# Decode attention: which queues load the paged cache (SP and POOL together, or SP alone)

## The reference, cut to what matters

```python
def mla_sample(x, cache_ckv, cache_kpe, page_table, ...):
    past_ckv = cache_ckv[page_table].reshape(B, -1, MLA_KV_LORA)   # 16 pages of 128 x 256 per batch
    past_kpe = cache_kpe[page_table].reshape(B, -1, MLA_ROPE)      # 16 pages of 128 x 64 per batch
    ...
    s = (einsum('bthr,bkr->bhtk', q_lat, all_ckv) + einsum('bthd,bkd->bhtk', q_pe, all_kpe)) * MLA_SCALE
    p = softmax(where(key_idx <= q_idx, s, -inf))
    o_lat = einsum('bhtk,bkr->bthr', p, all_ckv)
```

## Time and profile before

| | |
|---|---|
| time, median of 3 runs | 2721.86 us (2720.53 to 2725.43) |
| the profiled execution: its time / its span | 2732.0 us / 2730.3 us |
| mean granted TensorE clock | 0.938 |
| PE busy | 2497.6 us (91%) |
| DVE / ACT / POOL busy | 1053.8 us (39%) / 783.3 us (29%) / 1011.8 us (37%) |
| DMA, mean over the span | 76 GB/s |

### The profile page before, as it was taken

One profiled execution on the slowest core, in us unless ns is written; L12 is line 12 of the kernel. 1 busy time (PEld: TensorE's weight loads), 2 busy tenths in 40 slices (PEclk: granted clock), 3 DMA queues, 4 the chain that ended last, 5 costly groups with the idle time before them and its releaser, 6 DMA issues.

```text
span 2730.3 us, 45462 instructions
## 1 busy us (share of the span) xinstructions
PE 2497.6 (91%) x17472; PEld 2350.1 (86%) x17472; DVE 1053.8 (39%) x1953; ACT 783.3 (29%) x1323; POOL 1011.8 (37%) x596
## 2 busy tenths in 40 slices
PE   7999997799899699999979999979989776999996
PEld 6999997784457699999969999978988676999996
DVE  5333115576232633321163331145676446333213
ACT  4222223214332332222242222233221124222221
POOL 5333334320312343334343333443575024333342
PEclk9999998899998799999989999988989587999998
DMA  3222222120641132222212222222212211222221
GB/s 121 85 85 77 79 85 66 35 94 1 195 130 47 39 93 81 80 81 79 72 62 82 80 84 77 80 62 71 60 49 78 77 54 47 85 83 82 76 81 60
DMA packets 66584, 208.52 MB, mean 76 GB/s; under 512 B 8268, under 2 KB 19021, under 8 KB 66094
## 3 DMA queue, kind: packets, MB, share of 16 engines
q1 hardware_dynamic: 63406, 196.58, 23.3%
q0 software_dynamic: 3072, 10.49, 1.4%
HBM read 199.22 MB, written 7.82 MB: 76 GB/s over the span
## 4 chain that ended last, share of the span: by engine, by line
PE 84%; DVE 10%; issue 3%; POOL 2%; ACT 1%; DMA 0%; POOLq 0%; SPq 0%; DVEq 0%; ACTq 0%
PE psum L1389 24%; PE psum L1391 23%; PE psum L1390 23%; DVE h L919 2%; DVE x_lo L902 2%; DVE y_ffn L915 1%; PE psum L1648 1%; PE psum L1827 1%; PE psum L1704 1%; PE psum L1817 1%; PE psum L1583 1%; PE psum L1632 1%; PE psum L1777 1%; DVE work L910 1%; POOL w_lo L769 1%
## 5 line engine op out<-in xcount | busy, mean ns | idle before, releaser
L769 POOL TENSOR_TENSOR w_lo<-raw,w_hi 128x1024 fp32r<-128x1024 f32 x331 | 799.4, 2416 | 1353.5 <-ACT w_hi L467 1353.3
L1389 PE MATMUL psum<-x_hi,w_hi 128*128 128x288 f32 x3568 | 1077.6, 302 | 67.2 <-DVE x_lo L902 40.4
L1391 PE MATMUL psum<-x_hi,w_lo 128*128 128x288 f32 x3568 | 1065.0, 298 | 0.0
L1390 PE MATMUL psum<-x_lo,w_hi 128*128 128x288 f32 x3568 | 1064.7, 298 | 0.0
L1389 PEld LDWEIGHTS psum<-x_hi,w_hi 128*128 128x128 f32 x3568 | 683.7, 192 | 81.8 <-DVE x_lo L902 33.2
L1390 PEld LDWEIGHTS psum<-x_lo,w_hi 128*128 128x128 f32 x3568 | 684.0, 192 | 1.5
L1391 PEld LDWEIGHTS psum<-x_hi,w_lo 128*128 128x128 f32 x3568 | 682.9, 191 | 0.0
L467 ACT ACTIVATE w_hi<-raw 128x1024 fp32r<-128x1024 f32 x331 | 347.1, 1050 | 347.7 <-PE psum L1391 332.3
L1389 PE MATMUL psum<-gu_hi,w_hi 128*128 128x288 f32 x1408 | 418.7, 297 | 9.2 <-DVE gu_lo L953 9.2
L1391 PE MATMUL psum<-gu_hi,w_lo 128*128 128x288 f32 x1408 | 417.4, 296 | 0.0
L1390 PE MATMUL psum<-gu_lo,w_hi 128*128 128x288 f32 x1408 | 417.2, 296 | 0.0
(11 more groups left out here) (236 smaller groups left out, 2110.9 us busy)
## 6 DMA issues: line engine op xcount, KB each, us to landing
raw<-ffn_in SPq DMA_DIRECT2D x176, 512.0 KB, 3.6
raw<-ffn_out SPq DMA_DIRECT2D x64, 448.0 KB, 3.3
raw<-ffn_out SPq DMA_DIRECT2D x32, 512.0 KB, 3.5
raw<-gla_in SPq DMA_DIRECT2D x25, 512.0 KB, 3.6
cache<-cache SPq DMA_DIRECT2D x64, 160.0 KB, 3.1
cache<-cache POOLq DMA_DIRECT2D x64, 160.0 KB, 3.2
raw<-mla_wo SPq DMA_DIRECT2D x8, 512.0 KB, 3.6
raw<-gla_wo SPq DMA_DIRECT2D x8, 512.0 KB, 3.7
```

Source lines behind the costliest of these rows:

```text
L769: pool.tensor_tensor(w_lo[slot][:, :], raw[slot][:, :], w_hi[slot][:, :].bitcast(F32), ALU.subtract).then_inc(s_lo, 1)
L1389: pe.matmul(out, wh, xh, start=start, stop=False)
L1390: pe.matmul(out, wh, xl, start=False, stop=False)
L1391: return pe.matmul(out, wl, xh, start=False, stop=stop)
```

## The change

SP issues all four pages of each group and batch; the call on POOL goes, and with it the semaphores `s_cache_p`. TensorE waits for one semaphore that counts four pages instead of two that count two each. Nothing else in the order of any engine is changed.

```diff
@@ load_pages @@
-        def load_pages(eng, u0, landed, lo, hi):
+        def load_pages(eng, u0):
...
                     for b in (2 * bp, 2 * bp + 1):
-                        with eng.Fori(lo, hi) as i:
+                        with eng.Fori(0, 4) as i:
                             page = eng.value_load(table[0:1, bass.ds(PAGES * b + 4 * g + i, 1)], min_val=0,
                                                   max_val=N_POOL - 1)
                             eng.dma_start(cache[b % CACHES][:, 4 * g + i, :],
-                                          io["cache"][page]).then_inc(landed[b % CACHES][g], 16)
+                                          io["cache"][page]).then_inc(s_cache[b % CACHES][g], 16)
@@ SP, mla @@
-                load_pages(sp, u0, s_cache, 0, SP_PAGES)
+                load_pages(sp, u0)
@@ POOL, mla @@
-                load_pages(pool, first_unit[st], s_cache_p, SP_PAGES, 4)
@@ TensorE, transpose_pages @@
-                    pe.wait_ge(s_cache[b % CACHES][g], 16 * SP_PAGES * (b // CACHES + 1))
-                    pe.wait_ge(s_cache_p[b % CACHES][g], 16 * (4 - SP_PAGES) * (b // CACHES + 1))
+                    pe.wait_ge(s_cache[b % CACHES][g], 64 * (b // CACHES + 1))
```

More of the change, by code:

```diff
@@ L44 @@
 GROUPS = PAGES // 4
-SP_PAGES = 2
 CACHES = 4
@@ L231, in hybrid_step @@
         s_cache = [[sem(f"s_cache{i}_{g}") for g in range(GROUPS)] for i in range(CACHES)]
-        s_cache_p = [[sem(f"s_cache_p{i}_{g}") for g in range(GROUPS)] for i in range(CACHES)]
         s_tr, s_ctv, s_cta, s_score, s_snew = (sem(x) for x in ("s_tr", "s_ctv", "s_cta", "s_score", "s_snew"))
```

## The result

| | before | after |
|---|---|---|
| median of 4 runs | 2723.32 us (2720.53 to 2725.43) | 2787.73 us (2781.60 to 2794.35) |
| profiled execution: time / span | 2732.0 / 2730.3 us | 2787.0 / 2785.2 us |
| mean granted TensorE clock | 0.938 | 0.934 |

The ratio is 1.0238 (95% interval 1.0212 to 1.0264): slower by 2.4%. The two profiled executions differ by 55.0 us and the medians by 64.4.

The account below looks back on a forecast made before the run. TensorE bound the kernel before; after the change SP's issue rate was to bind. The attention's end shifts +62.6 us and the clock adds 4: 2721.9 + 66.6 = 2788.5 us, range 2774 to 2803.

Parts of the forecast that it names:

- POOL's loads removed, worth 0: On POOL: 64 page loads go, and nothing queued behind them could start earlier; worth 0.
- 128 loads of 1.53 us: On SP: 128 page loads in a row, 1.53 us each, the last issued at 882.3 us.
- No buffer wait: On SP at L343: buffers come free before their next pages are issued, so SP never waits and the stream is unbroken.
- TensorE waits in every step: In the attention: a pair needs 49 us of issuing against 35.2 of TensorE work, so the end follows the last page.
- Landing 2.8 us: Last group: 2.8 us from its last issue to TensorE's first transpose, so unit 31 begins at 885.1; bounds 2.1 and 3.1.
- The tail, 20.3 us at full clock: From unit 31's transposes to the last value product: keeps 20.3 us at the same clock; the end shifts by +62.6 us.
- the clock, +4: In the tail behind the last page: a low granted TensorE clock at first adds about 4 us; bounds 0 and 11.
- uv_f has room: On SP behind the last page: uv_f issued at about 884, needed at about 913; worth 0, with 24 us to spare.
- a constant shift: Behind the attention: everything from L1710 on was to be shifted by one constant.
- A: Rival for SP's page loads: SP alone reaches 1.10 us a page, loads stay hidden, 2714 to 2722 us; chance 0.03.
- B: Rival for SP's page loads: table read or DMA instruction gets faster without POOL, 1.3 us a page, 2759 us; chance 0.04.
- C: Rival on SP's queue: with 128 loads the DMA instruction begins to block, 1.9 us a page, 2836 us; chance 0.03.

Follow-up runs that it names:

- e4: Kernel after the change with all 128 page loads issued by POOL and none by SP; median 2795.0 us, ratio 1.0254 to the kernel before.
- e9: Kernel after the change, unchanged, timed again beside more runs of the kernel before; median 2793.65 us, ratio 1.0238.
- e1: Kernel after the change without the table read of the page number, so other pages are loaded; median 2731.7 us, ratio 1.0012 to the kernel before.
- e5: Kernel after the change with SP's loop over a group's four pages written out; median 2741.3 us, ratio 1.0052 to the kernel before.
- e8: Kernel before with three pages of each group on SP and one on POOL, both loops written out; ratio 1.0012 to the kernel before.
- e6: Kernel before, two pages each on SP and POOL, with the page loops written out on both queues; ratio 0.9987 to the kernel before.
- e7: Kernel after the change with each page number read twice from the table; median 2857.7 us, ratio 1.0487 to the kernel before.

## Why the prediction was right

The forecast was 2788.5 us, +66.6; measured 2787.7, +64.4, and by the ratio of the later 20 runs +64.9. By its steps:

1. **POOL's loads removed, worth 0.** Right. The low half behind them came at 899.62, again just behind ACT's high half.
2. **128 loads of 1.53 us.** Measured 1.512; the last issue is at 880.03 instead of 882.3: -2.3 us.
3. **No buffer wait.** Right: none in SP's list.
4. **TensorE waits in every step.** Not in every one, but the sum is right: 16 waits on the matmuls in 11 of the 16 steps, 50.9 us, in the band of 40 to 60. The steps without one stand at the turn of a pair, where softmax and value products fill the time. The end follows the last page all the same. The DMA share was put at 0.37 and is 0.39.
5. **Landing 2.8 us.** Measured 882.30 - 880.03 = 2.3: -0.5 us. I had read 2.8 while two queues loaded at once; with one, the median fell to 2.2.
6. **The tail, 20.3 us at full clock, and 7. the clock, +4.** Unit 31 to L1706 is 904.96 - 882.30 = 22.66 us, so the clock cost 2.3 instead of 4: -1.7 us. The low stretch held the transposes and the first scores, as expected, but ended sooner than I had allowed.
8. **uv_f has room.** Right: issued at 880.59, used at 908.42.

So the end of the attention moved by 904.96 - 842.83 = +62.1 us, where 66.6 was forecast. Within the profiled executions more of it was then given back. The stretch behind the attention, before and after (columns as in rows 2), and the start of the vector work that follows the output projection:
```profile
846.30:853.40 7.10, 7.01 (x32) 6.82 (x32) 0.00 (x0) 0.05 (x1) 0.00 (x0) 0.50 0.00 0
853.40:866.00 12.60, 11.28 (x67) 11.28 (x68) 2.23 (x5) 3.33 (x5) 2.55 (x2) 0.74 0.16 44
908.40:912.20 3.80, 3.76 (x32) 3.64 (x32) 0.00 (x0) 0.00 (x0) 0.00 (x0) 1.00 0.00 0
912.20:925.00 12.80, 11.41 (x86) 11.41 (x87) 3.19 (x7) 3.83 (x6) 4.80 (x2) 1.00 0.13 42
```
```profile
906.10 1.96 DVE work L910
962.60 1.96 DVE work L907
```
L1717 took 3.76 us at full clock, against 7.01 at the low one, and gave back 3.3 us; the output projection behind it began at a granted clock of 1.00 instead of 0.74 and gave back 2.4. So the shift is 56.5 us at 962.60 and 54.9 at the end. I had called this stretch a constant shift, and it was not. It is no accident of one execution: these matmuls took 3.8 us in e4 and e9 too, and 7.1 in e1, e5 and e8. The profiled execution was forecast at 2798.6 and had 2787.0. That the median came within 1 us of the forecast is therefore partly luck: three terms were too high by 4.5 us together, the give-back behind the attention was missing from the sum, and the runs lose more than the profiled pair shows. Only the issue rate, 194 us of the row of loads, was sized closely.

**A reading that was wrong.** The six instructions of the loop that the prediction calls the longest, 0.92 us together, leave out the register instruction of L348 with 79 ns (shown at e5), which is longer than three of them. All nine have medians of 1.05 us together, so the gaps between are some 0.45 us. The sum rests on the measured interval and does not change.

**The rivals.** A (the two queues slow each other, the loss vanishes) and B (something in between) fell with the interval of 1.512 us: SP alone is no faster than beside POOL. There is a threshold such as A named, though nearer 1.04 than 1.10 us (e5), and e1 shows what lies beyond it. C (the queue backs up) fell: the longest DMA instruction of 128 took 0.416 us.

**The two rules.** The Trainium skill ("DMA: Bandwidth & Descriptors", "Issuing engines are not separate DMA queues") says that DMAs issued by different engines run on the same 16 DMA engines. e1 agrees with it as far as it goes: one queue alone carried the pages as fast as TensorE needed them. That the sequencer's part is "usually small relative to the DMA itself" does not hold here: a page costs the sequencer 1.51 us and the 16 DMA engines 0.58 us (38.8% of 192 us for 128 pages). The floor of about 600 ns that the Trainium skill gives for a tensor_load (the same page, "Latency and other measured facts") is close to what one read costs in all in this loop (0.55 to 0.60 us, with the register work and the gaps behind it), though the instruction itself takes 0.27.

## What to carry to other kernels

For many small transfers with computed addresses, count the issuing sequencer's instructions, not the bytes: loads in the stretch times the interval on one queue, against the time that the consumer needs for the same data. For the end of the work, count the time up to the last load and not the average of a round (1.04 against 1.10 us here). Below that limit a second issuer is worth little (e1 and e8: 3.3 us each); above it, the end moves by the excess times the number of loads. Before adding or removing an issuer, write the loop out: here that took 0.39 of 1.51 us a page, for no change in the order. It gained time only where the loads were late: 51 us with SP alone, 1 to 3.5 us with two queues (e6).

## What was not expected

- Every 52 loads in the kernel after, four successive intervals grow by 0.2 to 0.35 us (1.85, 1.83, 1.74, 1.74 at loads 48 to 52; 1.83, 1.77, 1.71, 1.72 at loads 100 to 104). They cost about 2 us in all. In e9 they come at the same loads; in e7, with 12 instructions a page instead of 9, they come every 40 loads. 13 loops of four pages in the one and 10 in the other are the same length of program: counting each loop's body and the instruction that opens it, 13 x 10 and 10 x 13 are both 130. That they follow the program's length is argued from this count; no run tests it.
- Loop bookkeeping is dear on a sequencer. In e5 the counter, the branch and one register instruction go, some 0.14 us by their medians, another register instruction and the DMA instruction are 0.05 us shorter together, and the interval falls by 0.39: half of what was saved is time between instructions.
- The landing was shorter with less traffic, 2.2 us instead of 3.1, and longer with more (e6), 3.6 us, at DMA shares in the first pair of 0.39, 0.74 and 0.89. It does not follow the share alone: e5, with one queue, had 2.2 us at 0.53.
- By the ratios the runs lose 2 to 7 us more than the start of unit 31 moves in the profiles, in every version but e6 (e1 3.3 against 0.3, e5 14.2 against 9.2, after 64.8 against 59.8). Where this lies was not found.
- A difference of single profiles can be off by 10 us in this kernel. The time of a run goes with its mean granted clock: the 54 runs of the kernel before beside the experiments reach from 2718.2 us at 0.945 to 2733.7 at 0.937, the nine of the kernel after from 2781.6 at 0.936 to 2794.5 at 0.928. The profiled execution before, 2732.0 us at 0.938, stands near the slow end of its kernel and 8.7 us over its first median; the one after, 2787.0 us at 0.934, stands near the fast end of its own and 0.7 us under its median. These two make up the 9.4 us between 55.0 and 64.4. Why the clock differs from run to run is not shown. Inside the attention the profiles repeat well: from the first load to unit 31 it is 194.24 us in the kernel after and 194.22 in e9.
